# First gate weights in a place of their own, the split slot in two transfers, and the branch of the general path ahead of the last down products

## The reference, cut to what matters

```
mix  = (sigmoid(ga) * (o_a @ w_up_a) + sigmoid(gb) * (o_b @ w_up_b)) @ w_out
h    = h + mix
hf   = rmsnorm(h, norm2_g)
# one of 4 groups per row, then 2 of the group's 8 experts, with weights w
for each of the 32 experts e, for the rows that chose it:
    y = (silu(x @ w_gate[e]) * (x @ w_up[e])) @ w_down[e]     # 1024 -> 512 -> 1024
    h[row] += y * w
out  = rmsnorm(h, final_g)
```

## Time and profile before

| what | before |
|---|---|
| median of three runs | 1599.74 us |
| the profiled execution's own time | 1599.36 us |
| its span, first to last instruction | 1597.3 us |
| PE busy | 1570.2 us (98%) |
| DVE busy | 896.0 us (56%) |
| ACT busy | 192.5 us (12%) |
| moved by DMA | 374.68 MB, mean 235 GB/s |
| expert stage on PE | from 1156 us on |

### The profile page before, as it was taken

The page is one execution under the profiler, slowest core; times in us unless marked ns, Lnnn a source line. Parts: engine busy times, 40 slices in busy tenths (PEclk is TensorE's granted clock), DMA queues, the critical chain, the costliest instruction groups (busy, mean ns, idle before and its releaser), DMA issues.

```text
span 1597.3 us, 20637 instructions
## 1 busy us (share of the span) xinstructions
PE 1570.2 (98%) x8777; PEld 998.8 (63%) x8777; DVE 896.0 (56%) x1549; ACT 192.5 (12%) x311; POOL 36.0 (2%) x60
## 2 busy tenths in 40 slices
PE   8999999999999999999999999999999999999997
PEld 4866499974458564999744876899533333333332
DVE  5896766764659876676646676795432223121122
ACT  1321000000114110000001331410000000000001
POOL 1001000000010010000000000000000000000000
PEclk9999999999999999999999999999999999999999
DMA  6532545562534326355426333446999999999997
GB/s 213 204 106 105 181 145 164 169 216 105 212 103 162 106 105 217 114 167 184 178 105 247 122 106 132 158 173 262 376 411 426 425 424 428 426 425 427 428 421 302
DMA packets 129780, 374.68 MB, mean 235 GB/s; under 512 B 17220, under 2 KB 65672, under 8 KB 116888
## 3 DMA queue, kind: packets, MB, share of 16 engines
q1 hardware_dynamic: 118864, 370.62, 60.9%
q10 hardware_dynamic: 10824, 2.72, 0.7%
HBM read 372.28 MB, written 1.05 MB: 234 GB/s over the span
## 4 chain that ended last, share of the span: by engine, by line
PE 87%; DMA 10%; DVE 1%; SPq 1%; issue 0%; ACT 0%; POOL 0%; POOLq 0%; DVEq 0%
PE bank L870 16%; PE bank L1182 16%; PE bank L801 10%; PE bank L1619 10%; PE bank L813 6%; PE bank L1665 5%; PE bank L1435 4%; PE bank L1385 3%; DMA h<-in_w_down 3%; DMA turned_rows<-in_w_down 3%; DMA turned_rows<-in_w_gate 2%; PE bank L1307 2%; PE bank L1165 2%; PE bank L1468 2%; PE bank L1317 2%; PE bank L821 2%
## 5 line engine op out<-in xcount | busy, mean ns | idle before, releaser
L801 PE MATMUL bank<-weights,turned_rows 128*128 128x512 f32 x384 | 169.3, 597 | 0.4 <-DVE turned_rows L2118 0.4
L3265 DVE TENSOR_TENSOR bc<-mix,bank 128x512 f32<-128x512 f32 x16 | 17.3, 1079 | 216.1 <-PE bank L1619 216.1
L870 PE MATMUL bank<-arena 128*128 128x512 f32 x296 | 133.2, 592 | 0.0
L801 PEld LDWEIGHTS bank<-weights,turned_rows 128*128 128x128 f32 x384 | 72.5, 192 | 86.3 <-issue 85.8
L1182 PE MATMUL bank<-arena 128*128 128x128 f32 x960 | 110.5, 275 | 0.0
L1182 PEld LDWEIGHTS bank<-arena 128*128 128x128 f32 x960 | 108.8, 192 | 0.0
L870 PEld LDWEIGHTS bank<-arena 128*128 128x128 f32 x296 | 56.0, 190 | 69.9 <-issue 67.9
L813 PE MATMUL bank<-turned_rows,weights 128*128 128x256 f32 x448 | 98.6, 380 | 0.0
L813 PEld LDWEIGHTS bank<-turned_rows,weights 128*128 128x128 f32 x448 | 84.6, 190 | 12.1 <-issue 0.7
L1619 PE MATMUL bank<-arena,rows_late 128*64 128x512 f32 x248 | 88.8, 595 | 1.0 <-DMA weights<-in_w_up 0.6
L1665 PE MATMUL bank<-arena,mix 128*32 128x512 f32 x480 | 79.6, 594 | 2.4 <-DMA weights<-in_w_down 1.5
(11 more groups left out here) (540 smaller groups left out, 2553.8 us busy)
## 6 DMA issues: line engine op xcount, KB each, us to landing
weights<-in_w_in SPq DMA_DIRECT2D x28, 2048.0 KB, 8.1
arena<-in_w_gate SPq DMA_DIRECT2D x13, 2048.0 KB, 23.7
arena<-in_w_up SPq DMA_DIRECT2D x12, 2048.0 KB, 35.3
weights<-in_w_ffn_gate SPq DMA_DIRECT2D x22, 1024.0 KB, 5.4
weights<-in_w_ffn_up SPq DMA_DIRECT2D x22, 1024.0 KB, 8.3
weights<-in_w_ffn_down SPq DMA_DIRECT2D x10, 2048.0 KB, 7.9
arena<-in_w_down SPq DMA_DIRECT2D x10, 2048.0 KB, 30.8
weights<-in_w_up SPq DMA_DIRECT2D x9, 2048.0 KB, 20.8
```

What stands on the lines that cost most here:

```text
L801: ins = mm(b[:, :], xT[:, k, t0 + P * t:t0 + P * t + P], w[:, k, :], start=(k == 0), stop=(k == KD - 1))
L870: ins = mm(b[:, :], lhs[:, j, :], rhs[:, j, :], start=(first and j == 0), stop=(last and j == pairs - 1))
```

## The change

- Load 0 (gate weights of pair 0's first expert) leaves extra_slot. It goes to first_place, three regions used for it alone: 1024 KB in rows_late, 512 KB in the final gain's rows of bc (yE's new home), 512 KB at the start of mflat. It is issued as three DMAs behind load 6 and the first part of load 9, and counted on semaphore x_loaded0, for which PE waits before the first gate products.
- Load 11 goes to extra_slot at the point where load 0 was issued. The first refill step brings only load 12, still in four parts. REFILL_PARTS changes for loads 15 and 16, which now go in four parts.
- Place 9 lies in two parts of 1024 KB (split_part with twice the size, and h); yE moves from the arena to the final gain's rows of bc.
- Pair 0's rows are put into xsE[0] in place of xsE[1], and the dropped squares of half 0 go to h[:, 0, :].
- On PE the branch on n_passes stands ahead of the down products of pair 15. Their code and that of the last sums is there twice, once ahead of the general path's loop and behind it, once in the Else. DVE's copy of pair 15's first half and ACT's copy of its second half stand in both arms as well; ACT loads n_passes before its copy for pair 14.

```diff
-REFILL_PARTS = (4, 4, 2, 2, 2, 2, 2, 2)
+REFILL_PARTS = (4, 4, 2, 2, 4, 4, 2, 2)
...
-        yE = c.take(D)
-        split_part = c.take(2 * DE)
+        split_part = c.take(4 * DE)
+        yE = bc[:, BC2["fin"][0]:BC2["fin"][0] + D]
...
-        split_slot = ((0, 2, split_part), (2, 2, bc[:, BC2["fin"][0]:BC2["fin"][0] + D]), (4, 4, h.rearrange("p t n -> p (t n)")))
+        split_slot = ((0, 4, split_part), (4, 4, h.rearrange("p t n -> p (t n)")))
+        first_place = ((0, 4, rows_late[:, 0:4 * DE]), (4, 2, yE), (6, 2, mflat[:, 0:2 * DE]))
...
-                    for at in (first, first + 1):
+                    for at in (first, first + 1) if first else (1,):
...
                 if ch == N_LOADS - 9:
-                    load(0)
+                    load(NXS)
...
-            split_load(SPLIT, split_slot[:2])
+            split_load(SPLIT, split_slot[:1])
+            for q, pieces, v in first_place:
+                sp.dma_start(v, wsrc[0][0][:, DE * q:DE * q + DE * pieces]).then_inc(sem("x_loaded0"), 16)
...
+                if isinstance(n, int) and LOAD_AT[n, c6] == 0:
+                    pe.wait_ge(sem("x_loaded0"), 16 * (1 + len(first_place)))
+                    return lambda q: piece_of(first_place, q)
...
             with pe.If(n_passes > 1):
+                last_down()
                 with pe.Fori(1, n_passes) as turn:
                     with pe.Fori(0, PAIRS) as i:
                         pair(turn * PAIRS + i)
-            pe.wait_ge(sem("pickT_ready"), n_passes * PAIRS)
-            for half in range(2):
-                pe.wait_ge(sem(f"y_ready{half}"), n_passes * PAIRS)
-                for ins in sum_half(half, False):
-                    ins.then_inc(sem("sum_done"), 1)
+                last_sums(n_passes * PAIRS)
+            with pe.Else():
+                last_down()
+                last_sums(PAIRS)
```

More of the change, by code:

```diff
@@ L437, in program, with piece_of @@
         fin = ring_slots[2][:, 0:D]
+        def piece_of(places_, q):
+            first_q, _, v = [part for part in places_ if part[0] <= q < part[0] + part[1]][0]
+            return v[:, DE * (q - first_q):DE * (q - first_q) + DE]
         def weight_piece(at, q):
             if at == SPLIT:
-                first_q, _, v = [part for part in split_slot if part[0] <= q < part[0] + part[1]][0]
-                return v[:, DE * (q - first_q):DE * (q - first_q) + DE]
+                return piece_of(split_slot, q)
             return expert_slot[at][:, DE * q:DE * q + DE]
@@ L448, in program @@
             parts = 1
-            if i % NXS == SPLIT:
+            if i == 0:
+                parts = 0
+            elif i % NXS == SPLIT:
                 parts = len(split_slot)
-            elif NXS <= i < NXS + len(REFILL_PARTS):
+            elif NXS < i < NXS + len(REFILL_PARTS):
                 parts = REFILL_PARTS[i - NXS]
@@ L662, in _ @@
             sp.wait_ge(sem("m2_ready"), 4)
-            split_load(SPLIT, split_slot[2:])
+            split_load(SPLIT, split_slot[1:])
             sp.wait_ge(psum_full(ROUTE_TILE[1]), fills(ROUTE_TILE[1]))
@@ L1595, in rows_of_pair @@
             def rows_of_pair(n):
-                if not isinstance(n, int) or n == 0 or n == PAIRS - 1:
+                if not isinstance(n, int) or n == PAIRS - 1:
                     return xsE[1], 0
+                if n == 0:
+                    return xsE[0], 0
                 return xsE[(n - 1) // 2 % 2], SLOTS2 * ((n - 1) % 2)
@@ L1742, in _, with last_down, last_sums @@
             pe.wait_ge(sem("pickT_ready"), PAIRS)
-            for k in range(KE):
-                for half in range(2):
[L1745 to L1751, removed]
+            def last_down():
+                for k in range(KE):
+                    for half in range(2):
+                        if half == 0 or k == KE - 1:
+                            pe.wait_ge(sem(f"last_down{k + half}"), 32)
+                        ins = down(PAIRS - 1, w_last, half, k, last_hidT, 0)
+                        if k == KE - 1:
+                            ins.then_inc(sem("y_full"), 1)
+                    if k == 0:
+                        sum_up(PAIRS - 2, False, late_pickT)
+            def last_sums(pairs):
+                pe.wait_ge(sem("pickT_ready"), pairs)
+                for half in range(2):
+                    pe.wait_ge(sem(f"y_ready{half}"), pairs)
+                    for ins in sum_half(half, False):
+                        ins.then_inc(sem("sum_done"), 1)
             def pair(n):
@@ L2066, in _, with second_half_back @@
                 pair(i, True)
-            for i in (PAIRS - 2, PAIRS - 1):
+            def second_half_back(i, b):
                 act.wait_ge(sem("y_full"), 2 * i + 2)
-                act.activation(yE[:, 512:1024], moe_bank[3 if i < PAIRS - 1 else 1][:, :], ACT.Copy).then_inc(sem("y_ready1"), 1)
+                act.activation(yE[:, 512:1024], moe_bank[b][:, :], ACT.Copy).then_inc(sem("y_ready1"), 1)
             act.wait_ge(sem("passes_ready"), 1)
             n_passes = act.value_load(passes[0:1, 0:1], min_val=1, max_val=MAX_PASSES)
+            second_half_back(PAIRS - 2, 3)
             with act.If(n_passes > 1):
+                second_half_back(PAIRS - 1, 1)
                 with act.Fori(1, n_passes) as turn:
@@ L2075, in _ @@
                         pair(turn * PAIRS + i, False)
+            with act.Else():
+                second_half_back(PAIRS - 1, 1)
             for i in range(2 * NT):
@@ L3125, in rows_merged @@
                     v.sem_inc(psum_free(TILE["wo2"] + 2 * t + half), 1)
-                nc.vector.tensor_tensor_reduce(out=mflat[:, 1024 * t:1024 * t + 1024], in0=xn[:, t, :], in1=xn[:, t, :], scale=1.0, scalar=0.0,
+                nc.vector.tensor_tensor_reduce(out=(h[:, 0, :], mflat[:, 1024:2048])[t], in0=xn[:, t, :], in1=xn[:, t, :], scale=1.0, scalar=0.0,
                                                op0=ALU.mult, op1=ALU.add, accum_out=st1[:, t:t + 1]).then_inc(sem("dve_step"), 1)
@@ L3244, in pick_weights, with rows_in @@
                 ins.then_inc(sem("pickw_ready"), 1)
-            def rows_in(n):
+            def rows_in(n, xs=xsE[1]):
                 for q in range(2):
                     v.wait_ge(sem("xs_full"), n * 2 + q + 1)
-                    TT(xsE[1][:, 4 * q:4 * q + 4, 0:SLOTS2], moe_bank[2 + q][:, 0:4 * SLOTS2].rearrange("p (k n) -> p k n", k=4),
+                    TT(xs[:, 4 * q:4 * q + 4, 0:SLOTS2], moe_bank[2 + q][:, 0:4 * SLOTS2].rearrange("p (k n) -> p k n", k=4),
                        g2c[:, 4 * q:4 * q + 4].unsqueeze(2).to_broadcast([P, 4, SLOTS2]), ALU.mult).then_inc(sem("xs_ready"), 1)
@@ L3282, in rows_back @@
                     nc.vector.tensor_copy(yE[:, 512 * half:512 * half + 512], moe_bank[first_bank + half][:, :]).then_inc(sem(f"y_ready{half}"), 1)
-            rows_in(0)
+            rows_in(0, xsE[0])
             pick_rows(1, 4, 2)
@@ L3315, in _ @@
             rows_back(PAIRS - 2, (0,))
-            rows_back(PAIRS - 1, (0,), 0)
             with v.If(n_passes > 1):
+                rows_back(PAIRS - 1, (0,), 0)
                 with v.Fori(1, n_passes) as turn:
@@ L3329, in _ @@
                         rows_back(n_)
+            with v.Else():
+                rows_back(PAIRS - 1, (0,), 0)
             def gained(t, half):
```

## The result

The changed kernel takes 1605.05 us (median of six runs, 1604.06 to 1607.33) against 1599.84 for the kernel before in the same session (1599.31 to 1600.34): ratio 1.0033, 95% interval 1.0023 to 1.0044. (The ratios here aren't formed from the two medians and can differ a little from their quotient.) It is 5.2 us slower, and the forecast was 1.35 us faster, within a range up to 1601.2. The profiled execution took 1604.99 us, its span is 1602.8.

A forecast was written before the change was run, and what follows sets the result against it. The prediction took the end to be one stream of loads plus a tail of PE work. Stream -2.0, split slot -0.45, gap -0.4 and branch +1.5 summed to -1.35 us: median 1599.74 to 1598.4, range 1596.0 to 1601.2.

The forecast's parts named there:

- What bounds the kernel: Expert stage: PE sets the pace to about 1400 us, then waits on loads; the end is the load stream plus PE's tail.
- The twelfth place closes the hole at 1139: Load stream, 1139 to 1145: load 0, issued near 1119.9, fills 4.5 us left empty at 107 GB/s.
- The gain behind it, 2.0 of 4.9 us: Load stream behind 1142: 2.10 MB less to bring, worth 4.9 us if never dry; 2.0 taken, bounds 0.3 and 3.2.
- The two dry points: Load stream near 1167 and 1178: empty for 2.3 us and another 0.6 us, as PE frees slots no earlier.
- from there 4.19 MB in 4 KB rows at 410 GB/s: Loads 15 and 16 in quarters, from 1179.5: 10.2 us, through at 1189.7 instead of 1191.8, a gain of 2.1 us.
- The row of 349 GB/s at 1160: Rate of the earlier first quarters over 5 us; if new quarters keep it, 4.19 MB take 12.0 us, gain 0.3.
- The split slot, 0.45 us: Seven split-slot loads behind 1180: rows of 8 KB at 420 GB/s instead of 4 KB at 410 save 0.45 us.
- The gap before the last sums, -0.4: Between last down product and last sums: moving the branch removes the gap, -0.4 us, bounds -0.4 and 0.
- The branch as new wait, +1.5: PE ahead of the last down products: the jump's target must be fetched, +1.5 us, ends 0 and 2.6.
- 0.6 us from a branch's end to a packet: Fetch for the moved branch: 0.6 us until the code packet starts, plus 2.5 more, 3.1 us in all.
- The low clock: PE's last down products and sums: idle of 3.3 us would halve the clock, the 9.3 us left taking twice as long.
- rival E: Branch fetch over 4 us under full queues, clock falls to 1.2 GHz: -2.85 + 2.6 + 9.3, 1608.8 us; chance 8%.

The follow-up runs named there:

- places_only: Changed kernel with the branch and ACT's and DVE's copies back where they were, new places kept: 1599.11 us against 1600.31, ratio 0.9991.
- Halves: Changed kernel with PE's two arms exchanged and loads 15 and 16 in halves again: 1599.55 us against 1599.95 before, ratio 0.9994.
- branch_only: Kernel before with only the branch's part of the change (PE, ACT, DVE), places and loads untouched: 1606.57 us against 1600.31, ratio 1.0041.
- the kernel with 405 instructions: Changed kernel, general path's pair loop on PE replaced by 60 small products, so the branch jumps over 405 instructions: 1604.48 us against 1599.82, ratio 1.0030.
- the arms exchanged: Changed kernel with PE's one-turn path right behind the branch, general path in the Else: 1599.32 us against 1600.31 (0.9992); repeated, 1599.42 against 1599.95 (0.9999).
- The kernel with 165 instructions: Changed kernel with the general path's pair loop left out on PE, so the branch jumps over 165 instructions: 1598.98 us against 1600.31, ratio 0.9990.
- 289: Changed kernel, general path's pair loop on PE replaced by 31 small products, so the branch jumps over 289 instructions: 1599.17 us against 1599.82, ratio 0.9996.

## Why the prediction was wrong, point by point

- **What bounds the kernel**: right. The loads behind 1142 set the end, and PE follows the stream; in places_only it still waits for weights in six groups behind 1390.
- **The twelfth place closes the hole at 1139**: right. 414 GB/s in the changed kernel and 421 in places_only, where 107 were the earlier trace rows.
- **The gain behind it, 2.0 of 4.9 us**: the mechanism was right, the size too large. It measures 0.8 us in the changed kernel (counted as in the table above) and 0.5 to 1.2 in the others that keep the full clock at 1152. The two dry points are where they were forecast, and the second costs more. The kernel before moves 422 and 415 GB/s in these stretches. After:
```profile
1168.00:1171.00 3.00, 3.00 (x16) 1.01 (x14) 0.00 (x0) 0.00 (x0) 0.00 (x0) 1.00 0.62 164
1180.00:1186.00 6.00, 6.00 (x30) 2.01 (x28) 0.00 (x0) 0.60 (x1) 0.00 (x0) 1.00 0.86 268
```
  3 x (1 - 164/420) = 1.8 and 6 x (1 - 268/420) = 2.2 us of the stream are lost, 4.0 in place of 2.3 + 0.6 (2.9 to 4.2 in the other kernels with this refill). The step that failed is "from there 4.19 MB in 4 KB rows at 410 GB/s": the issues came where they should, but the rate was low.
```profile
1178.98 0.33 SPq L607 DMA_DIRECT2D arena<-in_w_down  x1
...
1184.13 0.33 SPq L607 DMA_DIRECT2D arena<-in_w_down  x1
```
  The row of 349 GB/s at 1160 that I set aside, for the 410 of the late quarters, was the nearer one: both stretches have quarters that arrive at a queue nearly empty, while the late ones arrive at a full one. (That this is the reason for the low rate wasn't tried by itself.) Halves lose it otherwise: their row below shows the queue as good as empty for 3 x (1 - 117/420) = 2.2 us; behind it they move 399 GB/s.
```profile
1179.00:1182.00 3.00, 3.00 (x16) 1.00 (x14) 0.00 (x0) 0.00 (x0) 0.00 (x0) 1.00 0.46 117
```
- **The split slot, 0.45 us**: right, 0.5. The Trainium skill ("DMA: Bandwidth & Descriptors", Specifications) gives 512 B as the smallest transfer for line rate. By that the term would have been 0, since rows of 4 and 8 KB are both far above it; the traces show 0.5.
- **The gap before the last sums, -0.4**: right against the profiled execution (-0.38), but it isn't a gain of the change: places_only hasn't moved the branch and has no gap either.
- **The branch as new wait, +1.5**: the mechanism was right, and this is the term that turned the sign. It measures 3.81 us of wait and 1.65 us of low clock, 5.5 together. The step that failed is "0.6 us from a branch's end to a packet". I took it from 1587.6, where the load queues were nearly done and no jump waited for the packet, and let "the queues are full there" count for 0.3 us. It was 3.6 us from the branch's start to the packet. "2.5 us from its start until it can be used" was right (2.6).
- **The low clock** was put at nothing in the sum; it stood in rival E and had 8%. Its condition came true: PE without a multiply for 4.5 us (4.9 in branch_only and 4.5 in the kernel with 405 instructions, both with the same low stretch; the other nine executions have neither there). Its price of 9.3 us was too high, since the clock was back after 3.4 us: 1.65.
- Sum by measured terms: -0.65 at the last landing, +3.81, +1.65, -0.38 are +4.4 us, for a measured +5.2 (1604.06 to 1607.33); the rest is within the spread of the front.

Of the 1.35 us that the stream of the changed kernel is ahead, 0.65 reach the landing of the first last-down piece. The stream itself doesn't lose the rest: it is still 1.4 us ahead at 1580. Before the piece has landed 0.3 MB more has come in than in the kernel before, which is 0.7 us at 410 GB/s. Why the piece lies further back among the others is open.

No version here clearly beats the kernel before. The nearest are the places with the branch left where it was (0.9991, up to 1.0000) and with the arms exchanged (0.9992, up to 1.0001; 0.9999, up to 1.0008, the second time). The kernel with 165 instructions (0.9990, up to 0.9999) lacks the loop that other inputs need.

## What to carry to other kernels

Before a branch is moved, count the code between it and its target on that engine and see where the code packets start in the trace: here a target in the packet already fetched cost 0.4 us, one packet further 3.3 to 3.7 us with idle DMA engines and 6.15 us behind full ones, and the idle time of 4.5 to 4.9 us was followed by 3.4 us at half the clock each time. Put the arm that is taken right behind the branch. And a place won is worth only what the next place's freeing leaves of it: one more slot closed a hole of 4.5 us, and about 3 to 4 of them opened again 25 to 45 us later.

## What the runs showed of the hardware that was not expected

- The price of a jump has a step between 289 and 405 instructions (378 and 6155 ns), at a place that is, by the count of the expectations, 140 to 200 instructions behind a packet's boundary.
- A code packet started 3.6 us behind a jump under full load queues (three executions), and 1.0 to 1.3 us behind one with idle DMA engines (five).
- Low clock also comes earlier, without a long idle time ahead of it: in four of the twelve profiled executions the granted clock was 0.50 for 3.4 us in the routing stretch, as in this one of the exchanged arms, while the stretch ahead of it was at 1.00. PE has a single wait there, 0.26 us for DVE near 1147, and has the same one in the executions that keep their clock. It costs 0.6 us at the first gate products. All four have the new places (four of ten; none of the two without them); whether the change makes it more frequent is open.
```profile
1145.00:1151.90 6.90, 6.62 (x46) 5.25 (x45) 3.58 (x11) 2.42 (x3) 0.55 (x1) 1.00 1.01 426
1151.90:1155.30 3.40, 3.40 (x18) 3.40 (x18) 1.93 (x11) 0.00 (x0) 0.00 (x0) 0.50 0.97 412
```
